# Where the residual joins the last product, and the order in which banded attention starts

## The reference

```
y  = rms_norm(x2, norm_final_g)          # residual of the second block
xn = rms_norm(y, norm_g_2)
q, k, v, z = split(xn @ w_in)            # 16 query heads of 64, 4 key/value heads
s  = q.k * 64**-0.5 + t5_bias            # window of 128 keys: own block and the one before
p  = softmax([s, sink])[..., :-1]
o  = (p @ v) * silu(z)
x3 = y + o @ w_out
return rms_norm(x3, final_g)
```

## Time and profile before

| what | value |
|---|---|
| median of 3 runs | 1234.31 us |
| profiled execution, device time | 1234.64 us |
| its span in the trace | 1232.8 us |
| PE busy | 1218.2 us, 99% of the span |
| DVE busy | 833.5 us, 68% |
| ACT busy | 495.4 us, 40% |
| granted TensorE clock | 0.999 of full |

### The profile page before, as it was taken

How to read it: one execution, slowest core, us unless ns; L and a number is a source line. 1 busy time by engine, 2 the same in 40 slices (tenths; PEclk the granted TensorE clock), 3 DMA queues, 4 the chain that set the end, 5 groups by cost and what they waited for, 6 DMA issues and landing times.

```text
span 1232.8 us, 16256 instructions
## 1 busy us (share of the span) xinstructions
PE 1218.2 (99%) x5836; PEld 1008.1 (82%) x5836; DVE 833.5 (68%) x1272; ACT 495.4 (40%) x786; POOL 20.6 (2%) x24
## 2 busy tenths in 40 slices
PE   8999999999999999999999999999999999999998
PEld 7988888888888888888888888888888888877776
DVE  7848797797789987554357866666654444467874
ACT  7543333322333324642234533434433333155553
POOL 4000000000000000000000000000000000000000
PEclk9999999999999999999999999999999999999999
DMA  8432232222222232252322323322243534211111
GB/s 315 144 124 97 85 102 86 86 86 80 74 86 88 99 103 100 72 180 94 102 98 74 103 102 102 102 86 92 95 138 103 206 103 171 86 52 53 67 54 68
DMA packets 35762, 128.07 MB, mean 104 GB/s; under 512 B 4016, under 2 KB 5072, under 8 KB 35456
## 3 DMA queue, kind: packets, MB, share of 16 engines
q1 hardware_dynamic: 33120, 116.41, 28.1%
q0 software_dynamic: 1296, 8.62, 2.0%
q10 hardware_dynamic: 1296, 2.36, 0.5%
HBM read 125.25 MB, written 5.27 MB: 106 GB/s over the span
## 4 chain that ended last, share of the span: by engine, by line
PE 94%; DVE 3%; ACT 2%; issue 1%; DMA 1%; SPq 0%; DVEq 0%; ACTq 0%
PE acc L839 78%; PE acc L856 4%; PE acc L1172 1%; PE acc L909 1%; PE side L1172 1%; PE acc L1141 1%; DVE w_low L1206 1%; PE side L1112 1%; PE acc L873 1%; PE acc L1125 1%; PE side L978 1%; PE side L998 1%; DMA w_raw<-weights 1%; ACT w_high L463 0%; DVE x L1760 0%
## 5 line engine op out<-in xcount | busy, mean ns | idle before, releaser
L839 PE MATMUL acc<-h_high,w_high 128*128 128x512 f32 x880 | 342.8, 390 | 0.0
L839 PE MATMUL acc<-h_high,w_low 128*128 128x512 f32 x880 | 342.4, 389 | 0.0
L839 PE MATMUL acc<-h_low,w_high 128*128 128x512 f32 x880 | 342.4, 389 | 0.0
L1206 DVE TENSOR_TENSOR w_low<-w_raw,w_high 128x1024 fp32r<-128x1024 f32 x214 | 264.0, 1245 | 44.5 <-ACT w_high L463 41.3
L463 ACT ACTIVATE w_high<-w_raw 128x1024 fp32r<-128x1024 f32 x214 | 222.1, 1051 | 104.6 <-PE acc L839 91.0
L839 PEld LDWEIGHTS acc<-h_high,w_low 128*128 128x128 f32 x880 | 165.2, 188 | 34.3
L839 PEld LDWEIGHTS acc<-h_low,w_high 128*128 128x128 f32 x880 | 165.2, 188 | 34.2
L839 PEld LDWEIGHTS acc<-h_high,w_high 128*128 128x128 f32 x880 | 165.2, 188 | 34.0
L1274 DVE SCALAR_TENSOR_TENSOR convs<-long_u,par,convs 128x510 f32<-128x510 f32 (+28 forms) x232 | 170.3, 734 | 6.6
L839 PE MATMUL acc<-f_high,w_high 128*128 128x512 f32 x176 | 68.6, 390 | 0.0
L839 PE MATMUL acc<-f_low,w_high 128*128 128x512 f32 x176 | 68.5, 389 | 0.0
(11 more groups left out here) (314 smaller groups left out, 1894.6 us busy)
## 6 DMA issues: line engine op xcount, KB each, us to landing
w_raw<-weights SPq DMA_DIRECT2D x214, 512.0 KB, 3.2
rows_dram<-strip_dram POOLq DMA_DIRECT2D x1, 3072.0 KB, 14.9
x_in<-x SPq DMA_DIRECT2D x4, 512.0 KB, 7.7
x<-x POOLq DMA_DIRECT2D x1, 2048.0 KB, 8.6
bias<-rows_dram POOLq DMA_DIRECT2D x1, 2048.0 KB, 12.4
w_raw<-weights SPq DMA_DIRECT2D x8, 128.0 KB, 5.8
mem_in<-mem ACTq DMA_DIRECT2D x4, 256.0 KB, 6.6
out<-result SPq DMA_DIRECT2D x4, 256.0 KB, 2.0
```

What stands on the lines that cost most here:

```text
L839: mm = pe.matmul(acc[:, bank, 0:width], w[:, s, (skip + b) * P:(skip + b + 1) * P], moving[v][:, k, :], start=first and b == 0 and w is w_ ...
L1206: dve.tensor_tensor(w_low[:, s, :], raw[s][:, :], w_high[:, s, :].bitcast(F32), ALU.subtract)\
```

## The change

The residual stays in columns. After the product (R_QKV, 3) PE spreads the root of the first normalisation over `side` bank 3 (four fp32 matmuls with the identity), and DVE makes `y_cols` = x2 * gain * root, eight tiles 128x512, two in each of four slots. All `turn_x`, `y_rows`, `g_final_rows` and its DMA are gone.

A new `residual(t)` opens the banks of tile t: for both halves, four fp32 matmuls `y_cols` block by identity, the first with start=True. Tiles 2 and 3 go after the last half product of z and ahead of `outputs(7)`; tiles 0 and 1 inside k = 0, just ahead of their own matmuls. All matmuls of `last` then accumulate. DVE's add (L1760) and `x3` are gone; ACT squares straight from PSUM; the two sums join in the root (the first half's mean is its bias); DVE takes the reciprocal after it and scales the second half straight from PSUM with the gain.

Before the steps the order is now V tile 0, `scores(0)`, `scores(1)`, V tiles 1 and 2, `scores(2)`, V tile 3. `ahead(R_Z, 0)` moves on DVE behind `normalised(1)` and `biased(2)`, on ACT behind `exps(2)` of step 0.

The diff, cut to its core (left out: names of semaphores, buffers that only change name or go, the input array of gains):

```diff
@@ -156,8 +156,7 @@
         bias = sb("bias", [P, HEADS_B, 2 * P], F32, 113)
-        y_rows = sb("y_rows", [P, 4, D], F32, 97)
-        g_final_rows = sb("g_final_rows", [P, D], F32, 177)
+        y_cols = sb("y_cols", [P, KT, SEQ], F32, 97)
         g_last_rows = sb("g_last_rows", [P, D], F32, 113)
@@ -775,7 +775,6 @@
                     v.then_inc(taken[2 + t // 2], 1)
-            ahead(R_Z, 0)
             for step in range(2 * KT):
@@ -790,6 +789,7 @@
                     exps(2)
+                    ahead(R_Z, 0)
                 if step + 3 < 2 * KT:
@@ -806,20 +806,19 @@
                 for half in range(2):
-                    act.wait_ge(x3_done, 2 * t + half + 1)
-                    if t or half:
-                        act.wait_ge(x3_squared, 2 * t + half)
-                    act.activation(square[:, half, :], x3[:, t, half * SEQ:(half + 1) * SEQ], ACT.Square,
+                    act.wait_ge(last_done, 2 * t + half + 1)
+                    act.activation(square[:, half, :], last_bank(t, half), ACT.Square,
                                    accum_out=last_sum[:, t, half:half + 1]).then_inc(x3_squared, 1)
-                act.wait_ge(last_step, 2 * t + 2)
-                act.activation(last_root[:, t:t + 1], last_sum[:, t, 3:4], ACT.Sqrt, scale=float(D))\
-                   .then_inc(last_rooted, 1)
-                act.wait_ge(last_rooted, t + 1)
-                act.wait_ge(x3_gained, 2 * t + 2)
-                act.activation(result[:, t, SEQ:D], result[:, t, SEQ:D], ACT.Copy, scale=last_root[:, t:t + 1])\
+                act.wait_ge(x3_squared, 2 * t + 2)
+                act.wait_ge(last_bias, t + 1)
+                act.activation(last_root[:, t, 0:1], last_sum[:, t, 1:2], ACT.Sqrt, scale=1.0 / D,
+                               bias=last_sum[:, t, 2:3]).then_inc(last_rooted, 1)
+                act.wait_ge(last_inverse, t + 1)
+                act.wait_ge(x3_gained, t + 1)
+                act.activation(result[:, t, 0:SEQ], result[:, t, 0:SEQ], ACT.Copy, scale=last_root[:, t, 1:2])\
                    .then_inc(result_other, 1)
                 act.wait_ge(result_other, t + 1)
-                act.dma_start(out[t * P:(t + 1) * P, SEQ:D], result[:, t, SEQ:D]).then_inc(stored, 16)
+                act.dma_start(out[t * P:(t + 1) * P, 0:SEQ], result[:, t, 0:SEQ]).then_inc(stored, 16)
@@ -1077,25 +1076,17 @@
-            def turn_x(n):
-
-                t, half = n // 2, n % 2
-                at_least(pe, y_ready, n - 1)
-                for c in range(4):
-                    mm = pe.transpose(side[:, n % 2, c * P:(c + 1) * P], x2[:, 4 * half + c, t * P:(t + 1) * P], ident)
-                mm.then_inc(y_turned, 1)
-
             product(R_QKV, 3, xn)
+            pe.wait_ge(root_done, N_FINAL + 3)
+            for t in range(SEQ // P):
+                mm = pe.matmul(side[:, 3, t * P:(t + 1) * P], root_col[:, t:t + 1].broadcast_to((P, P)), ident,
+                               start=True, stop=True)
+            mm.then_inc(final_ready, 1)
             for s in range(SLOTS):
-                turn_x(s)
                 product(R_QKV + 1, s, xn)
             for s in range(2):
-                turn_x(4 + s)
                 product(R_QKV + 2, s, xn)
-            turn_x(6)
             rows(R_QKV + 2, 2, xn, 4, range(1))
-            turn_x(7)
-            rows(R_QKV + 2, 2, xn, 4, range(1, 2))
@@ -1125,6 +1116,14 @@
                 mm.then_inc(sw_turned, 1)
+
+            def residual(t):
+
+
+                for half in range(2):
+                    for c in range(4):
+                        pe.matmul(last_bank(t, half)[:, c * P:(c + 1) * P],
+                                  y_cols[:, 4 * half + c, t * P:(t + 1) * P], ident, start=c == 0, stop=False)
@@ -1150,8 +1149,9 @@
             scores(1)
-            rows(R_QKV + 2, 2, xn, 4, range(2, 4))
+            rows(R_QKV + 2, 2, xn, 4, range(1, 3))
             scores(2)
+            rows(R_QKV + 2, 2, xn, 4, range(3, 4))
             for s in range(2, SLOTS):
@@ -1162,18 +1162,21 @@
                         used=uses(R_Z, 0) + j)
+                if step == 2 * KT - 1:
+                    pe.wait_ge(sw_step, 6 * 2 * KT)
+                    for t in (2, 3):
+                        residual(t)
                 if step % 2 == 1:
-                s, bank = k % 4, (acc if t < 2 else side)[:, 2 * (t % 2) + half, :]
+                s, bank = k % 4, last_bank(t, half)
                 for o, w in ((o2_high, w_high), (o2_high, w_low), (o2_low, w_high)):
                     mm = pe.matmul(bank, o[:, k, t * P:(t + 1) * P], w[:, s, half * SEQ:(half + 1) * SEQ],
-                                   start=k == 0 and o is o2_high and w is w_high, stop=k == KT - 1 and o is o2_low)
+                                   start=False, stop=k == KT - 1 and o is o2_low)
                 return mm
-            pe.wait_ge(sw_step, 6 * 2 * KT)
             for k in range(LAST_BY_TILE):
@@ -1184,6 +1187,8 @@
                         pe.wait_ge(taken[Z_BANK], uses(R_Z, 0) + KT)
+                    if k == 0 and t < 2:
+                        residual(t)
                     for half in range(2):
@@ -1656,17 +1661,13 @@
                             root_times(j)
-                        dve.wait_ge(root_done, N_FINAL + 3)
-                        dve.wait_ge(rows_landed, 16)
                     if 2 <= k < KT + 2:
                         root_times(k)
-                    if 4 <= k:
-                        n = k - 4
-                        dve.wait_ge(y_turned, n + 1)
-                        t, at = n // 2, SEQ * (n % 2)
-                        dve.scalar_tensor_tensor(y_rows[:, t, at:at + SEQ], side[:, n % 2, :], root_col[:, t:t + 1],
-                                                 g_final_rows[:, at:at + SEQ], ALU.mult, ALU.mult)\
-                           .then_inc(y_ready, 1)
+                    if k == 4:
+                        dve.wait_ge(final_ready, 1)
+                    for n in ((2 * (k - 4), 2 * (k - 4) + 1) if 4 <= k < 8 else ()):
+                        dve.scalar_tensor_tensor(y_cols[:, n, :], x2[:, n, :], col("g_final", n), side[:, 3, :],
+                                                 ALU.mult, ALU.mult).then_inc(y_ready, 1)
             dve.wait_ge(bias_landed, 16)
@@ -1751,26 +1752,18 @@
                 ahead(R_LAST + s // 4, s % 4)
-            dve.wait_ge(rows_landed, 32)
+            dve.wait_ge(rows_landed, 16)
             for t in range(4):
-                for half in range(2):
-                    n, at = 2 * t + half, SEQ * half
-                    dve.wait_ge(last_done, n + 1)
-                    bank = (acc if t < 2 else side)[:, 2 * (t % 2) + half, :]
-                    dve.tensor_tensor(x3[:, t, at:at + SEQ], bank, y_rows[:, t, at:at + SEQ], ALU.add)\
-                       .then_inc(x3_done, 1)
-                    dve.wait_ge(x3_done, n + 1)
-                    dve.tensor_tensor(result[:, t, at:at + SEQ], x3[:, t, at:at + SEQ], g_last_rows[:, at:at + SEQ],
-                                      ALU.mult).then_inc(x3_gained, 1)
-                dve.wait_ge(x3_squared, 2 * t + 2)
-                dve.tensor_scalar(last_sum[:, t, 2:3], last_sum[:, t, 0:1], last_sum[:, t, 1:2], EPS * D,
-                                  ALU.add, ALU.add).then_inc(last_step, 1)
-                dve.wait_ge(last_step, 2 * t + 1)
-                dve.reciprocal(last_sum[:, t, 3:4], last_sum[:, t, 2:3]).then_inc(last_step, 1)
+                dve.wait_ge(x3_squared, 2 * t + 1)
+                dve.tensor_scalar(last_sum[:, t, 2:3], last_sum[:, t, 0:1], 1.0 / D, EPS, ALU.mult, ALU.add)\
+                   .then_inc(last_bias, 1)
+                dve.tensor_tensor(result[:, t, 0:SEQ], last_bank(t, 0), g_last_rows[:, 0:SEQ], ALU.mult)\
+                   .then_inc(x3_gained, 1)
                 dve.wait_ge(last_rooted, t + 1)
-                dve.wait_ge(x3_gained, 2 * t + 2)
-                dve.tensor_scalar(result[:, t, 0:SEQ], result[:, t, 0:SEQ], last_root[:, t:t + 1], None, ALU.mult)\
-                   .then_inc(result_ready, 1)
+                dve.reciprocal(last_root[:, t, 1:2], last_root[:, t, 0:1]).then_inc(last_inverse, 1)
+                dve.wait_ge(last_inverse, t + 1)
+                dve.scalar_tensor_tensor(result[:, t, SEQ:D], last_bank(t, 1), last_root[:, t, 1:2],
+                                         g_last_rows[:, SEQ:D], ALU.mult, ALU.mult).then_inc(result_ready, 1)
```

More of the change, by code:

```diff
@@ L170, in build @@
         o2_low = sb("o2_low", [P, KT, SEQ], F32R, 48)
-        x3 = sb("x3", [P, 4, D], F32, 80)
         result = sb("result", [P, 4, D], F32, 153)
@@ L193, in build @@
         last_sum = sb("last_sum", [P, 4, 4], F32)
-        last_root = sb("last_root", [P, 4], F32)
+        last_root = sb("last_root", [P, 4, 2], F32)
         small = sb("small", [P, 6, 4], F32)
@@ L315, in build @@
         rows_landed = sem("rows_landed")
-        y_turned = sem("y_turned")
+        final_ready = sem("final_ready")
```

(15 more changed lines are left out.)

## The result

The changed kernel takes 1238.03 us (median of seven, 1237.9 to 1239.21) against 1234.31 us (seven, 1233.94 to 1234.65): a ratio of 1.0032, 95% interval 1.0023 to 1.0042, so 3.7 us slower. The profiled execution took 1238.33 us with a span of 1236.5 us, against 1234.64 and 1232.8. The granted clock is 0.999 as before.

What follows compares the result with a forecast made beforehand. PE was taken as the bound, with 94% of the span. Terms -2.64 + 0.89 + 2.2 + 3.4 + 0.8 - 1.2 = +3.45, say +3.5 us, on 1234.31 gave 1237.8 us; range 1235.4 to 1240.2.

Steps and rivals of the forecast that it cites:

- case A: The forecast itself for the whole kernel: +3.5 us, 1237.8 us, chance 0.60.
- Transposes out, spread in: Ahead of V tile 0 on PE: six groups of transposes removed, -2.64 us; four fp32 matmuls spreading the root, +0.89 us.
- The residual's passes: 32 fp32 identity matmuls, two passes of 0.101 us each: 3.3 us ahead of `outputs(7)`, 3.4 us inside k = 0.
- Case C: Rival: PE does a matmul by the identity at a transpose's price; +0.35 us, 1234.7 us, chance 0.06.
- Hidden part: Ahead of `outputs(7)`: PE's 1.1 us wait for DVE hides part of the residual's 3.3 us, leaving +2.2 us.
- Start of attention: Up to the first outputs: +0.8 us, two removed transposes included; PE waits 1.8 us on V copies, 1.1 ahead of outputs.
- Rival B: Start of attention costs nothing, no extra wait of the first outputs: shift -0.3 there, +2.4 us in all, 1236.7; chance 0.16.
- Tail: From the last matmul's start to the last DMA's issue: 3.60 us becomes 2.4 us, -1.2 us.
- The 4× of the page: Rival for the residual's matmuls: each costs four times a transpose, +7.4 us, 1245.2 us, chance 0.01.

## Why the prediction was right

Forecast 1237.8 us, measured 1238.03; case A. Step by step:

- *Transposes out, spread in.* Forecast -1.75, measured -2.0 us. The spread is 0.89 us as read from L1076. Each group of transposes cost a little more than its 0.44 us, since the product behind it lost time at the change of form: such a product took 5.49 us, and 32.68 / 6 = 5.45 us now.
- *The residual's passes.* Forecast 3.3 and 3.4 us; measured 3.57 and 3.56 (twice 1.78). The pitch is 0.11 us instead of 0.101 (3.57 / 32). The spread's eight records were too few to tell the pitch from what the change of form costs; with 0.89 / 8 = 0.11 I would have had it. That a matmul by the identity isn't priced as a transpose decided whether the change loses anything that can be measured, and the runs without the residual (-5.8 us of span) and with transposes (half) show it. Case C, the transpose's price, is what its run then measured as a kernel of its own: 1234.95 us, C's number having been 1234.7.
- *Hidden part.* 1.1 us of the first group, by the wait ahead of `outputs(7)`: gone in the trace after, back in the run without the residual.
- *Start of attention.* Forecast +0.8, measured +0.7; both waits came out as written, 1.8 and 1.1 us. The splitting holds as well: the chain through `ahead` is the last link of the second wait, and costs 0.3 us more than the old one did; the rest is PE's order. Rival B, a relief because `normalised(1)` and `biased(2)` left the chain, fails on what took their place, w_low and `biased(3)`.
- *Tail.* -1.2 us up to the last issue, forecast and measured, and again when undone. But the prediction took what follows the issue as unchanged ("The last DMA is still ACT's, of the same size"), and it isn't: SP's store now lands last, and issue to end is 3.14 us instead of 2.83. The tail as a whole is worth 0.9 us.
- *Luck.* The sum is nearer than its terms. Two misses made the kernel faster than forecast: the first stage saved 0.25 us more, and the profiled execution reached L1069 0.15 us earlier. Three made it slower: 0.3 and 0.1 us at the residual, and the 0.3 us at the end, for which the sum had nothing. That they nearly cancel is luck. The mechanism of each large term is what the runs show.

The 4× of the page cited in the prediction (the Trainium skill, "TensorE: Matmul & The Clock Gate", section Terms) is not what this case shows: 3.57 to 1.75 us for the same 16 blocks, a factor of 2.04.

## What to carry to other kernels

Before a value is added in PSUM by a product with the identity, read the price of that form in the trace: in fp32 the plain matmul takes two passes here, the transpose mode one, and the mode can open the sum just as well. When PE is the bound, a step of another engine that leaves the chain is worth only what the next wait lets through: look what then stands at the head of each queue, and what used to cover the wait. And nothing covers a chain at the very end, but measure it to the end of the span and not to the last issue: here 1.2 us up to the issue were 0.9 at the end.

## What the runs showed of the hardware that was not expected

A group of transposes slows the product behind it too: the product's second start came 0.32 us after the first (1043.40 and 1043.72 us in the trace before) instead of 0.23, and six products with no such group before them took 0.04 us less each (5.45 instead of 5.49). After the fp32 spread at L1076 it was 0.31 us (1037.48 and 1037.79). And a bank opened by fp32 transposes (start on the first of four, none on the rest) takes the sums of ordinary fp32r matmuls on top, as the run with transposes has it, at 0.11 us a block. Last, two stores of 256 KB landed 2.0 and 2.5 us after their issues when they were issued 0.24 us apart, and 2.8 and 2.6 us when 0.03 us apart.
